# Experts' weights in pairs of units into a ring of six pairs, and the experts' outputs spread over the tokens on the chip

## The chip, the cores and the metric

One core of a Trainium2 chip. The metric is the device time of one execution in microseconds, as the median of three runs. All tensors are float32 in memory.

## The reference

Two layers of a decoder on 256 tokens of width 1024. Layer 0 is a gated DeltaNet and a dense SwiGLU, layer 1 a stick-breaking attention and a mixture of eight SwiGLU experts of which each token takes two. After each of the four parts stands a LayerNorm of `alpha * x + part(x)`. The change is in the last part:

```python
logits = xt @ router
top_val, top_idx = lax.top_k(logits, 2)
gates = softmax(top_val)
combine = sum_k(one_hot(top_idx, 8) * gates[..., None])
for e in range(8):                       # w_gate, w_up: 1024 x 3584, w_down: 3584 x 1024
    y = y + combine[:, e:e+1] * ((silu(xt @ w_gate[e]) * (xt @ w_up[e])) @ w_down[e])
h = layer_norm(alpha * h + y, g, b)
```

The experts' weights are 336 MiB.

## The kernel before

Weights come in units of 1 MiB, 128 partitions by 2048 float32. An expert is 42 units: of gate, up and down columns in four chunks (GATE, UP and DOWN give where a chunk's units stand in the round). Eight rounds run one expert each, in turn **heavy** (up to 128 rows of tokens, rounds 0, 2, 4, 6) and **light** (up to 64 rows, rounds 1, 3, 5, 7). The first heavy round is written out, then a loop of three bodies has a light and a heavy round each, and the last light round follows.

*Heavy round.* Each product is made of three f32r matmuls of high and low halves. ScalarE copies a landed unit into a high half (`hi`, line 737, and `next_hi`, 1245, six buffers), VectorE subtracts it from the unit in place, which leaves the low half in the ring (`lo`, line 2174; `los`, 2847), and TensorE multiplies (`wide_part`, 1994, `deep`, 1443; lines 1349 to 1351 are the three matmuls, 12 to a unit). TensorE's order (`heavy_round`, 2009) is gate of chunk 0 (four units), up of chunk 0 (four), two units of gate 1, `turned(0)` (transposes of silu(gate) times up, which VectorE makes in `gate_times_up`, 2835), and so on. VectorE's order is `heavy_round`, 2851: low halves 6 to 11, `gate_times_up(0)`, low half 12, ...; halves 0 to 5 are made at the end of the light round.

*Light round.* Plain fp32 matmuls straight from the landed unit, on two 64-column halves of the array at once (line 2080), with no high and low halves.

*The ring.* SyncE issues the loads in order (`units_in`, 529, issue at line 540). Twelve slots of one unit each hold the experts' weights. Unit j waits until TensorE has used unit j - 12 (`unit_used`); the first twelve wait for the dense part instead. Between the last two down chunks SyncE loads the next round's token rows from `by_slot` in HBM into `rows_io` (`slot_rows`, 518).

*Outputs.* At the start of a round ScalarE copies the round before's output out of PSUM with the gate as scale and writes it to `by_slot` in HBM (`heavy_sent`, 1206, one transfer of 512 KiB; `light_sent`, 1213, two of 128 KiB, behind four `next_hi`). When the fourth heavy output and the third light one have landed (`y_landed`), GpSimd gathers each token's two rows in four indirect transfers of 128 rows of 1024 and adds them to x (lines 697 to 719), during the last light round. The last light round's output goes another way: TensorE brings x into PSUM by the identity and adds the output by a 0/1 matrix `back` (128 rows by 256 tokens), split in Yh and Yl (`scatter`, 1973). Then the last LayerNorm (`last_norm`, 2790) reads PSUM, and five transfers store the result.

Of the kernel before, what the change touches and what calls it, by code (L numbers as in the profile page):

```python
# [21 lines left out]
ds = bass.ds  # L22
# [92 lines left out]
def hybrid_trunk(nc, x, gdn_w_in, gdn_conv_w, gdn_a_log, gdn_dt_bias, gdn_norm_w, gdn_w_out,  # L115
                 sb_w_in, sb_w_out, ffn_w_gate, ffn_w_up, ffn_w_down,
                 moe_router, moe_w_gate, moe_w_up, moe_w_down, ln_g, ln_b, out):
    with ExitStack() as ctx:
# [8 lines left out]
        raw_low = sb("raw_low", [P, RAW, UNIT], F32R, overlaid)  # L127
# [3 lines left out]
        w_lo_raw = sb("w_lo_raw", [P, SPLIT, UNIT], F32, overlaid)  # L131
        overlaid.close()
# [61 lines left out]
        def group(t, gr):  # L194
# [18 lines left out]
        w_lo_more_raw = sb("w_lo_more_raw", [P, DEEP - SPLIT, UNIT], F32, overlaid)  # L213
        overlaid.close()
# [23 lines left out]
        last_rows = ExitStack()  # L238
        Yh = sb("Yh", [P, 512], F32R, last_rows)
        Yl = sb("Yl", [P, 512], F32R, last_rows)  # L240
        last_rows.close()
# [6 lines left out]
        back = sb("back", [P, SEQ], F32R, fm)  # L248
# [29 lines left out]
        backs = sb("backs", [P, TOPK * NT], F32, fm)  # L278
        backi = sb("backi", [P, TOPK * NT], I32, fm)
# [33 lines left out]
        gdn_in = raw_in[RAW:RAW + GRAW]  # L313
        x_back = sem("x_back")
# [27 lines left out]
                  for k in range(3)]  # L342
# [28 lines left out]
        back_done, yh_done, yl_done = sem("back_done"), sem("yh_done"), sem("yl_done")  # L371
        y_sent, light_y_sent, y_landed, x_scaled, x_summed = (sem(n) for n in ("y_sent", "light_y_sent", "y_landed", "x_scaled", "x_summed"))
        y_got = [sem(f"y_got{i}") for i in range(2)]
# [18 lines left out]
        def split_slot(j):  # L392

            if U_FFN <= j < U_SBIN + 2:
                return (j + 1) % DEEP
            return j % DEEP if j >= U_MOE else j % SPLIT

        def unit_hi(j):
            s = split_slot(j)
            return w_hi[:, s, :] if s < SPLIT else w_hi_more[:, s - SPLIT, :]  # L400

        def ring_slot(j):
            return (j - U_MOE) % RING

        def ring(j, first, second, third):

            s = ring_slot(j)
            if s < RAW:
                return first[:, (s + U_MOE - U_FFN + GRAW) % RAW, :]
            return second[:, s - RAW, :] if s < RAW + SPLIT else third[:, s - RAW - SPLIT, :]  # L410

        def unit_lo(j):
            if j >= U_MOE:
                return ring(j, raw_low, w_lo, w_lo_more)
# [7 lines left out]
        def raw_slot(j):  # L422

            if j >= U_MOE:
                return ring(j, raw, w_lo_raw, w_lo_more_raw)
# [2522 lines left out]
```

## Time and profile before

| | |
|---|---|
| median of three runs | 1493.82 us (1492.81 to 1495.9) |
| the profiled execution | 1492.33 us |
| its span, first to last instruction | 1490.6 us |
| TensorE busy | 1425.4 us (96%) |
| weight loads of TensorE busy | 1054.2 us (71%) |
| VectorE, ScalarE, GpSimd busy | 831.9, 695.8, 131.3 us |
| mean granted clock of TensorE | 0.991 |
| HBM read, written | 458.03 MB, 12.34 MB |

Busy is the time in which an engine had an instruction in work. In the slices of the span each digit is tenths of one fortieth of the span (37 us). The chain of waits follows the work that ended last back from the end of the program; its rows give start, length, engine, tile and line.

### The profile page before, as it was taken

The page shows a single profiled execution, that of the slowest core. Times are in us where ns is not written, and L with a number is a line of the kernel's source. Part 1 is how long each engine was busy: PE and PEld are TensorE (multiplying, and loading weights), DVE is VectorE, ACT ScalarE, POOL GpSimd, SP SyncE. Part 2 cuts the span into 40 slices and gives each one's busy share as a digit, 9 for nine tenths or more (in the row PEclk, how much of TensorE's full clock was granted, in tenths as well). Part 3 has the DMA queues.
Part 4 walks back from the last instruction along what each step waited for, and adds up shares of the span by engine and source line. Part 5 has one row for each costly group of instructions (what it writes and reads, how often), then busy time and mean ns, then how long its engine had stood idle before and what let it go on. Part 6 is the DMA issues. An engine that isn't in the chain of part 4 may idle for free.

```text
span 1490.6 us, 19514 instructions
## 1 busy us (share of the span) xinstructions
PE 1425.4 (96%) x7640; PEld 1054.2 (71%) x7640; DVE 831.9 (56%) x739; ACT 695.8 (47%) x686; POOL 131.3 (9%) x140
## 2 busy tenths in 40 slices
PE   9999999999999999999998899997899997999976
PEld 8899988888888898888833488632688533888322
DVE  6787667644454746899700499300798102997002
ACT  6755475444333455587500587300777102875001
POOL 1668110000000000004000000000000000000021
PEclk9999999999999999999999999999999999999998
DMA  8493238565545553699999999999999999999995
GB/s 292 133 346 113 89 102 318 173 212 183 196 169 185 193 168 132 231 378 385 419 413 421 421 421 421 422 422 421 422 422 421 422 422 422 422 422 421 420 420 229
DMA packets 104389, 471.25 MB, mean 316 GB/s; under 512 B 10484, under 2 KB 17160, under 8 KB 61320
## 3 DMA queue, kind: packets, MB, share of 16 engines
q1 hardware_dynamic: 99560, 459.01, 78.0%
q10 hardware_dynamic: 3392, 7.18, 1.3%
q0 software_dynamic: 1376, 4.22, 0.7%
q8 instruction: 42, 0.69, 0.2%
q14 instruction: 19, 0.16, 0.0%
HBM read 458.03 MB, written 12.34 MB: 316 GB/s over the span
## 4 chain that ended last, share of the span: by engine, by line
PE 72%; DMA 14%; POOL 5%; DVE 5%; issue 2%; ACT 1%; SPq 1%; POOLq 0%; ACTq 0%; DVEq 0%
PE ps L1349 17%; PE ps L1351 17%; PE ps L1350 17%; PE ps L2080 10%; DMA w_lo_more_raw<-in_moe_w_down 5%; DMA raw<-in_moe_w_gate 5%; DMA raw<-in_moe_w_down 3%; POOL X L654 2%; POOL ab L649 2%; PE ps L1383 1%; PE ps L1385 1%; PE ps L1386 1%; PE ps L1669 1%; PE ps L2036 1%; PE ps L1674 1%
## 5 line engine op out<-in xcount | busy, mean ns | idle before, releaser
L762 ACT ACTIVATE w_hi<-raw 128x2048 fp32r<-128x2048 f32 x105 | 198.8, 1913 | 63.8 <-PE ps L1386 28.8
L2176 DVE TENSOR_TENSOR w_lo<-raw,w_hi 128x2048 fp32r<-128x2048 f32 x67 | 153.6, 2305 | 62.3 <-ACT w_hi L762 60.7
L2897 DVE TENSOR_TENSOR hs<-hs,ps 128x512 f32<-128x512 f32 (+1 forms) x16 | 9.9, 622 | 318.6 <-PE ps L2080 318.6
L2176 DVE TENSOR_TENSOR raw_low<-raw,w_hi 128x2048 fp32r<-128x2048 f32 x48 | 108.9, 2288 | 58.8 <-ACT w_hi L1249 49.7
L762 ACT ACTIVATE w_hi_more<-raw 128x2048 fp32r<-128x2048 f32 x62 | 117.0, 1914 | 19.1 <-PE ps L1351 16.4
L2080 PE MATMUL ps<-raw,xs_light 128*64 128x512 f32 (+1 forms) x576 | 102.5, 501 | 12.3 <-DMA raw<-in_moe_w_gate 7.9
L2176 DVE TENSOR_TENSOR raw_low<-raw,w_hi_more 128x2048 fp32r<-128x2048 f32 x48 | 108.7, 2288 | 4.9 <-ACT w_hi_more L762 3.2
L1349 PE MATMUL ps<-w_hi,xeh 128*128 128x512 f32 x224 | 91.2, 407 | 15.0 <-DVE raw_low L2176 14.7
L2080 PEld LDWEIGHTS ps<-raw,xs_light 128*64 128x64 f32 x576 | 40.2, 137 | 72.1 <-issue 46.9
L1350 PE MATMUL ps<-raw_low,xeh 128*128 128x512 f32 x224 | 90.0, 402 | 0.0
L1351 PE MATMUL ps<-w_hi,xel 128*128 128x512 f32 x224 | 89.7, 401 | 0.0
L1349 PE MATMUL ps<-w_hi_more,xeh 128*128 128x512 f32 x224 | 87.5, 391 | 0.0
L1351 PE MATMUL ps<-w_hi_more,xel 128*128 128x512 f32 x224 | 87.2, 389 | 0.0
L2176 DVE TENSOR_TENSOR w_lo<-w_lo_raw,w_hi 128x2048 fp32r<-128x2048 f32 x36 | 81.4, 2289 | 10.0 <-ACT w_hi L762 9.7
L1290 ACT ACTIVATE h_light<-ps 128x512 f32<-128x512 f32 (+1 forms) x16 | 8.7, 544 | 161.0 <-PE ps L2111 161.0
L2176 DVE TENSOR_TENSOR w_lo_more<-w_lo_more_raw,w_hi_more 128x2048 fp32r<-128x2048 f32 x36 | 81.1, 2286 | 1.7 <-ACT w_hi_more L762 1.4
L762 ACT ACTIVATE w_hi_more<-w_lo_more_raw 128x2048 fp32r<-128x2048 f32 x36 | 69.1, 1920 | 20.7 <-PE ps L1351 12.2
L762 ACT ACTIVATE w_hi<-w_lo_raw 128x2048 fp32r<-128x2048 f32 x36 | 67.9, 1912 | 13.7 <-PE ps L1351 7.5
L2080 PE MATMUL ps<-w_lo_raw,xs_light 128*64 128x512 f32 x288 | 65.0, 595 | 2.8 <-DMA w_lo_raw<-in_moe_w_up 2.8
L1383 PE MATMUL ps<-xT0h,w_hi 128*128 128x256 f32 x224 | 64.9, 290 | 0.0
L706 POOL DMA_INDIRECT rows_io<-by_slot,backi x2 | 2.0, 1004 | 710.5 <-ACTq L1223 710.2
L1385 PE MATMUL ps<-xT0l,w_hi 128*128 128x256 f32 x224 | 64.0, 286 | 0.0
(449 smaller groups left out, 3294.0 us busy)
## 6 DMA issues: line engine op xcount, KB each, us to landing
raw<-in_moe_w_gate SPq DMA_DIRECT2D x56, 1024.0 KB, 16.4
raw<-in_moe_w_up SPq DMA_DIRECT2D x56, 1024.0 KB, 17.3
raw<-in_moe_w_down SPq DMA_DIRECT2D x56, 1024.0 KB, 14.4
w_lo_raw<-in_moe_w_up SPq DMA_DIRECT2D x32, 1024.0 KB, 18.0
w_lo_more_raw<-in_moe_w_gate SPq DMA_DIRECT2D x32, 1024.0 KB, 16.8
w_lo_raw<-in_moe_w_down SPq DMA_DIRECT2D x28, 1024.0 KB, 19.4
w_lo_more_raw<-in_moe_w_down SPq DMA_DIRECT2D x28, 1024.0 KB, 23.7
w_lo_raw<-in_moe_w_gate SPq DMA_DIRECT2D x24, 1024.0 KB, 12.3
```

The lines of the kernel that those rows point to most:

```text
L649: nc.gpsimd.tensor_tensor(tmp, blocks[:, j + 1:SUB, j:j + 1].broadcast_to([P, left, j + 1]), inv[:, j:j + 1, 0:j + 1].broadcast_to([P, lef ...
L654: nc.gpsimd.tensor_tensor(rest, rest, tmp, ALU.subtract).then_inc(sub_step, 1)
L762: nc.scalar.activation(unit_hi(j), raw_slot(j), ACT.Copy).then_inc(hi_done, 1)
L1349: nc.tensor.matmul(o, lh, rh, start=start, stop=False, skip_group_check=True)
L1350: nc.tensor.matmul(o, lh, rl, start=False, stop=False, skip_group_check=True)
L1351: return nc.tensor.matmul(o, ll, rh, start=False, stop=stop, skip_group_check=True)
L1383: nc.tensor.matmul(o, unit_hi(j)[:, w], xh[:, kk, :], start=kk == 0 and m % 2 == 0, stop=False, skip_group_check=True)
L1385: nc.tensor.matmul(o, unit_hi(j)[:, w], xl[:, kk, :], start=False, stop=False, skip_group_check=True)
L1386: last = nc.tensor.matmul(o, unit_lo(j)[:, w], xh[:, kk, :], start=False, stop=kk == KD - 1, skip_group_check=True)
L1669: last = nc.tensor.matmul(ps[:, bank, h * P:(h + 1) * P], lhs(h), rhs(h), start=True, stop=True)
L2080: last = nc.tensor.matmul(ps[half * HALF:half * HALF + HALF, bank, 0:width], tile, raw_slot(j)[:, w], start=start, stop=False, skip_group_ ...
L2176: V.tensor_tensor(unit_lo(j), raw_slot(j), unit_hi(j).bitcast(F32), ALU.subtract).then_inc(lo_done, 1)
```

## The change

The ring becomes six pairs of units: HBM holds the weights so that two units stand side by side, 16 KiB per partition, and one transfer loads both when both old units are used. The twelve slots lie in one piece of memory, over `raw`, `w_hi` and `w_lo`; the experts' high halves move to `w_hi_more` and `w_lo_more`. Outputs no longer go to HBM: ScalarE leaves them in `rows_io`, VectorE builds `back` for each round, TensorE multiplies both in plain fp32 into PSUM, one token tile at a time, and VectorE adds the tile to x. The four gathers, their index steps and the Yh/Yl split go. In the last round `residual` brings x into PSUM ahead of the last two units.

```diff
-        raw_low = sb("raw_low", [P, RAW, UNIT], F32R, overlaid)
+        ring_raw = sb("ring_raw", [P, RING, UNIT], F32, overlaid)
+        overlaid.close()
+        ring_low = sb("ring_low", [P, RING, UNIT], F32R, overlaid)
...
         def unit_hi(j):
+            if j >= U_MOE:
+                s = (j - U_MOE) % DEEP
+                return w_hi_more[:, s, :] if s < SPLIT else w_lo_more[:, s - SPLIT, :]
...
-            return (j - U_MOE) % RING
-        def ring(j, first, second, third):
-            s = ring_slot(j)
-            if s < RAW:
-                return first[:, (s + U_MOE - U_FFN + GRAW) % RAW, :]
-            return second[:, s - RAW, :] if s < RAW + SPLIT else third[:, s - RAW - SPLIT, :]
+            s = (j - U_MOE) % RING
+            return (s + U_MOE - U_FFN + GRAW) % RAW if s < RAW else s
...
+        def raw_pair(j):
+            s = ring_slot(j)
+            return ring_raw[:, s:s + 2, :].rearrange("p u n -> p (u n)")
...
+            def slot_rows(r, at, light):
                 if isinstance(r, int):
                     sp.wait_ge(K_pe.sem, K_pe.after("x1", r - 1))
                 else:
-                    sp.wait_ge(light_y_sent if light else y_sent, (32 if light else 16) * (i + 1))
+                    sp.wait_ge(y_spread, NT * (r - 1))
...
             def units_in(r, u, w, e, at, first, count):
-                for i in range(count):
+                for i in range(0, count, 2):
                     j = u + at + i
                     if not isinstance(r, int) or j >= U_MOE + RING:
-                        sp.wait_ge(unit_used, units(j - RING, FC * (r - (u != U_MOE))))
+                        sp.wait_ge(unit_used, units(j + 1 - RING, FC * (r - (u != U_MOE))))
                     elif j < U_MOE + RAW:
-                        sp.wait_ge(lo_done, units(j - RAW))
-                    elif j < U_MOE + RAW + SPLIT:
-                        sp.wait_ge(unit_used, units(j - RAW - SPLIT))
+                        sp.wait_ge(lo_done, units(j + 1 - RAW))
                     else:
-                        sp.wait_ge(mixed, SBH // 2)
-                    sp.dma_start(raw_slot(j), weight_unit(w, e, first + i)).then_inc(raw_sem(j), 16)
...
-            def heavy_sent(h, r):
+            def heavy_output(h, r):
                 act.wait_ge(unit_used, units(U_MOE + DOWN[3] + 1, FC * r))
                 nc.scalar.activation(rows_io[:], ps[:, 2:4, :].rearrange("p b n -> p (b n)"), ACT.Copy,
-                                     scale=gates(heavy_meta, h)).then_inc(yh_done, 1)
-                act.wait_ge(yh_done, r + 1)
-                act.dma_start(by_slot[ds(h * PAIR + HALF, P), :], rows_io[:]).then_inc(y_sent, 16)
...
+            def light_output(l, r):
                 act.wait_ge(unit_used, units(U_MOE + DOWN[3] + 1, FC * r))
+                nc.scalar.activation(rows_io[:, 0:512], ps[:, 2, :], ACT.Copy, scale=gates(light_meta, l)).then_inc(y_copied, 1)
...
             def heavy_round(h, r, l=None):
                 if l is not None:
+                    light_output(l + 1, r - 1)
                     for k in range(2, DEEP):
                         next_hi(r, k)
-                    light_sent(l, r - 1)
                 his(r, 6, 8)
...
+            def residual():
                 for t in range(NT):
                     for half in range(2):
-                        w = slice(half * 512, half * 512 + 512)
-                        o = ps[:, 4 + 2 * t + half, :]
-                        if t == 1:
-                            nc.tensor.matmul(o, IDENT, X[:, 1, w], start=True, stop=False)
-                    pe.wait_ge(yl_done, 1)
-                    for Y in (Yh, Yl):
-                        for half in range(2):
-                            rows = slice(half * HALF, half * HALF + HALF)
-                            last = nc.tensor.matmul(ps[:, 4 + 2 * t + half, :], back[rows, t * P:(t + 1) * P], Y[rows, :],
-                                                    start=False, stop=Y is Yl)
-                            if Y is Yl:
-                                last.then_inc(y_last, 1)
+                        nc.tensor.matmul(ps[:, 4 + 2 * t + half, :], IDENT, X[:, t, half * 512:half * 512 + 512], start=True,
+                                         stop=False)
+            def spread(rows, t, o, y, start):
+                return nc.tensor.matmul(o, back[rows, t * P:(t + 1) * P], y, start=start, stop=True)
+            def heavy_spread(r, t):
+                pe.wait_ge(y_copied, r + 1)
+                pe.wait_ge(back_done, r + 1)
+                if t:
+                    pe.wait_ge(x_added, NT * r + t)
+                for half in range(2):
+                    last = spread(slice(0, P), t, ps[:, 5 + 2 * half, :], rows_io[:, half * 512:half * 512 + 512], True)
+                last.then_inc(y_spread, 1)
+            def light_spread(r, t):
+                pe.wait_ge(y_copied, r + 1)
+                pe.wait_ge(back_done, r + 1)
+                if t:
+                    pe.wait_ge(x_added, NT * r + t)
+                for half in range(2):
+                    rows = slice(half * HALF, half * HALF + HALF)
+                    last = spread(rows, t, ps[:, 6 + half, :], rows_io[rows, 0:512], True)
+                last.then_inc(y_spread, 1)
+            def last_spread(r):
+                pe.wait_ge(y_copied, r + 1)
+                pe.wait_ge(back_done, r + 1)
+                for t in range(NT):
+                    for half in range(2):
+                        rows = slice(half * HALF, half * HALF + HALF)
+                        spread(rows, t, ps[:, 4 + 2 * t + half, :], rows_io[rows, 0:512], False).then_inc(y_last, 1)
...
                 for half in range(2):
                     rows_ready(h, r, half)
                     gate(0, (2 * half, 2 * half + 1))
+                if l is not None:
+                    light_spread(r - 1, 0)
                 up(0)
+                if l is not None:
+                    light_spread(r - 1, 1)
                 gate(1, (0, 1))
+                if l is not None:
+                    pe.wait_ge(x_added, NT * r)
                 turned(0)
                 gate(1, (2, 3))
                 up(1)
                 if l is not None:
-                    pe.wait_ge(yh_done, r)
+                    pe.wait_ge(y_copied, r)
                 down(0, range(4))
                 turned(1)
                 gate(2, range(4))
                     if c:
                         pe.wait_ge(light_act.sem, light_act.after(f"high{c - 1}", l))
...
                 gate(0, range(4))
+                heavy_spread(r - 1, 0)
                 up(0)
+                heavy_spread(r - 1, 1)
                 gate(1, (0, 1))
                 turned(0)
                 gate(1, (2, 3))
                 down(1, (2, 3))
                 gate(3, range(2))
                 up(3)
+                pe.wait_ge(x_added, NT * r)
                 if not last_round:
                     heavy_rows(r + 1)
                 down(2, (0, 1))
                 turned(3)
                 down(2, (2, 3))
+                if last_round:
+                    residual()
                 down(3, range(2))
             pe.wait_ge(R_dve.sem, R_dve.after("pick1"))
...
+            def tokens_of(meta, i):
+                ids = meta[:, i, 1:2] if isinstance(i, int) else meta[:, ds(i, 1), 1:2].rearrange("p a b -> p (a b)")
+                V.tensor_scalar(back[:], tokens[:], ids, None, ALU.is_equal).then_inc(back_done, 1)
+            def output_added(r, t, banks):
+                dve.wait_ge(y_spread, NT * r + t + 1)
+                x_t = X[:, t, :].rearrange("p (b n) -> p b n", b=2)
+                V.tensor_tensor(x_t, x_t, ps[:, banks, :], ALU.add).then_inc(x_added, 1)
...
             def heavy_round(h, r):
                 first = isinstance(h, int)
-                los(h, 6, 11)
+                if first:
+                    los(h, 6, 8)
+                else:
+                    output_added(r - 1, 0, slice(6, 8))
+                    los(h, 6, 8)
+                    output_added(r - 1, 1, slice(6, 8))
+                    tokens_of(heavy_meta, h)
+                los(h, 9, 11)
                 gate_times_up(h, r, 0, slice(4, 6))
                 los(h, 12, 12)
                 if first:
...
             def light_round(l, r, last=False):
+                for t in range(NT):
+                    output_added(r - 1, t, slice(5, 8, 2))
+                tokens_of(light_meta, 0 if last else l + 1)
                 for c in range(4):
...
-            scatter_matrix()
+            tokens_of(heavy_meta, 0)
+            dve.wait_ge(x_scaled, NT)
             with dve.Fori(0, n) as i:
                 light_round(i, 2 * i + 1)
                 heavy_round(i + 1, 2 * i + 2)
             light_round(n, 2 * n + 1, last=True)
-            output_lo(2 * n + 1)
```

## Rows read from the trace of the kernel before

**Rows 1.** The page, the span in 40 slices: DMA share in tenths, GB/s.
```profile
DMA  8493238565545553699999999999999999999995
GB/s 292 133 346 113 89 102 318 173 212 183 196 169 185 193 168 132 231 378 385 419 413 421 421 421 421 422 422 421 422 422 421 422 422 422 422 422 421 420 420 229
```

**Rows 2.** Windows: stretch, length, five engines' busy us, PEclk, DMA share, GB/s.
```profile
900.00:1000.00 100.00, 100.00 (x461) 61.97 (x461) 42.75 (x24) 36.35 (x26) 0.00 (x0) 1.00 1.01 422
80.00:84.00 4.00, 4.00 (x27) 3.59 (x26) 3.94 (x3) 2.03 (x6) 0.00 (x0) 1.00 1.09 385
```

**Rows 3.** The chain of waits, from 550 us: start, us, what.
```profile
746.65 17.32 PE ps L2080 x80
...
833.53 1.92 ACT w_hi L1249
...
957.80 17.32 PE ps L2080 x80
...
1045.96 1.92 ACT w_hi L1249
...
1171.39 17.32 PE ps L2080 x80
...
1258.46 1.92 ACT w_hi L1249
...
1383.43 17.32 PE ps L2080 x80
```

**Rows 4.** Timeline of TensorE in a heavy round: units 6 and 9 begin.
```profile
855.89 0.39 PE L1349 MATMUL ps<-w_hi,xeh 128*128 128x512 f32 x1
...
864.05 0.39 PE L1349 MATMUL ps<-w_hi_more,xeh 128*128 128x512 f32 x1
```

**Rows 5.** Waits of SyncE's queue: us in total, times, longest.
```profile
SPq L540 <- PE ps L1351: 426.7, 171, 18.6
```

**Rows 6.** Line 540, whole run, then 741:747, 950:958, 1165:1172.
```profile
DMA to landing us min/median/max: 4.7/16.0/29.4
...
DMA to landing us min/median/max: 6.1/6.3/6.6
...
DMA to landing us min/median/max: 9.0/9.1/9.5
...
DMA to landing us min/median/max: 7.5/8.0/8.4
```

**Rows 7.** DMA issues: count, KB each, median us to landing.
```profile
by_slot<-rows_io ACTq DMA_DIRECT2D x4, 512.0 KB, 7.9
...
by_slot<-rows_io ACTq DMA_DIRECT2D x6, 128.0 KB, 6.7
...
rows_io<-by_slot,backi POOLq DMA_INDIRECT x2, 8.8
hs<-by_slot,backi POOLq DMA_INDIRECT x2
```

**Rows 8.** Timeline of TensorE in `scatter`.
```profile
1475.66 1.98 PE L1977 MATMUL ps<-X,cst 128*128 128x512 f32 x4
...
1477.57 0.49 PE L1989 MATMUL ps<-Yh,back 64*128 64x512 f32 x2
```

**Rows 9.** VectorE's lines 2839, 2783, 2176: ns min/median/max.
```profile
L2839 DVE TENSOR_TENSOR hs<-hs,ps x16: 679/1213/1216, 650.8 to 1366.3; 128x1024 f32<-128x1024 f32 x12, 128x512 f32<-128x512 f32 x4
...
L2783 DVE TENSOR_SCALAR back<-tokens,light_meta x1: 353/353/353, 737.4 to 737.4; 128x256 fp32r<-128x256 f32 x1
...
L2176 DVE TENSOR_TENSOR raw_low<-raw,w_hi x48: 2281/2291/2294, 601.1 to 1360.4; 128x2048 fp32r<-128x2048 f32 x48
```

**Rows 10.** Timeline of the tail: last unit, its copy, statistics of tile 1.
```profile
1473.79 1.94 PE L2080 MATMUL ps<-w_lo_more_raw,h_light 128*64 128x512 f32 x8 [0.51 <-DMA w_lo_more_raw<-in_moe_w_down]
...
1475.77 0.69 ACT L1201 ACTIVATE Yh<-ps,light_meta 128x512 fp32r<-128x512 f32 x1 [9.16 <-PE ps L2080]
...
1480.91 0.70 DVE L2795 BATCH_NORM_STATS2 stats<-ps 128x6 f32<-128x512 f32 x1 [0.97 <-PE ps L1989]
```

More of the change, by code:

```diff
@@ L370, in hybrid_trunk @@
         K_dve = Stages(sem("K_dve"), ["l0", "l1"])
-        back_done, yh_done, yl_done = sem("back_done"), sem("yh_done"), sem("yl_done")
-        y_sent, light_y_sent, y_landed, x_scaled, x_summed = (sem(n) for n in ("y_sent", "light_y_sent", "y_landed", "x_scaled", "x_summed"))
-        y_got = [sem(f"y_got{i}") for i in range(2)]
+        back_done, y_copied, y_spread, x_scaled, x_added = (sem(n) for n in ("back_done", "y_copied", "y_spread", "x_scaled",
+                                                                            "x_added"))
         def by_halves(at):
@@ L402, in ring_slot @@
         def ring_slot(j):
[L403 to L410 removed]
+            s = (j - U_MOE) % RING
+            return (s + U_MOE - U_FFN + GRAW) % RAW if s < RAW else s
         def unit_lo(j):
             if j >= U_MOE:
[L414 removed]
+                return ring_low[:, ring_slot(j), :]
             s = split_slot(j)
@@ L558, in expert @@
                 if at is not None:
-                    next_rows(r, i, at, light)
+                    next_rows(r, at, light)
                 units_in(r, u, moe_w_down, e, DOWN[2], 8, 4)
@@ L755, in hi @@
                     act.wait_ge(unit_used, units(U_SBIN - 2 if j == U_SBIN + 2 else U_SBIN - 1))
-                elif j < U_MOE + SPLIT and first:
+                elif j < U_MOE and first:
                     act.wait_ge(unit_used, units(j - SPLIT))
@@ L1321, in _ @@
             n = act.value_load(idi[0:1, COUNT:COUNT + 1], min_val=BODIES, max_val=BODIES + MAX_OVER)
-            with act.Fori(n, TURNS):
-                act.sem_inc(y_landed, 2)
             with act.Fori(0, n) as i:
@@ L1327, in _ @@
             light_round(n, 2 * n + 1, last=True)
-            act.wait_ge(unit_used, units(U_MOE + DOWN[3] + 1, FC * (2 * n + 1)))
-            last_output()
+            light_output(0, 2 * n + 1)
             nc.scalar.activation(warm[:, 3], rw[:, 0, 0:1], ACT.Sqrt, scale=0.0)
@@ L1971, in first_rows @@
                 last.then_inc(K_pe.sem, 1)
-            def scatter():
-                pe.wait_ge(x_summed, TOPK * NT)
-                for half in range(2):
-                    nc.tensor.matmul(ps[:, 4 + half, :], IDENT, X[:, 0, half * 512:half * 512 + 512], start=True, stop=False)
-                pe.wait_ge(back_done, 1)
+            def residual():
                 for t in range(NT):
                     for half in range(2):
-                        w = slice(half * 512, half * 512 + 512)
-                        o = ps[:, 4 + 2 * t + half, :]
-                        if t == 1:
-                            nc.tensor.matmul(o, IDENT, X[:, 1, w], start=True, stop=False)
-                    pe.wait_ge(yl_done, 1)
-                    for Y in (Yh, Yl):
-                        for half in range(2):
-                            rows = slice(half * HALF, half * HALF + HALF)
-                            last = nc.tensor.matmul(ps[:, 4 + 2 * t + half, :], back[rows, t * P:(t + 1) * P], Y[rows, :],
-                                                    start=False, stop=Y is Yl)
-                            if Y is Yl:
-                                last.then_inc(y_last, 1)
+                        nc.tensor.matmul(ps[:, 4 + 2 * t + half, :], IDENT, X[:, t, half * 512:half * 512 + 512], start=True,
+                                         stop=False)
@@ L2878, in heavy_round @@
                 los(h, 26, 28)
-                if first:
-                    outputs_placed()
                 los(h, 29, 32)
```

105 lines of the change are left out of this document (24 added, 81 removed), and 2 rows, old and new, of the table R_dve.

## The prediction

> **What bounds the kernel now.** I read the page's slices first [rows 1]: in the experts' half, from about 690 us on, the DMA engines stand at 9 in every slice and move 413 to 422 GB/s, while TensorE's row also shows 9. Two engines that both look full call for a view by stage. A stretch inside the experts (first row of [rows 2]) has DMA at a share of 1.01 and 422 GB/s, so 1 MiB takes 2.49 us. The chain of waits [rows 3] shows how the two share the time. A heavy round runs from the moment its first unit has landed (833.53, 1045.96, 1258.46) to the first matmul of the next light round (957.80, 1171.39, 1383.43): 124.3, 125.4 and 125.0 us, mean 124.9. One heavy unit is 2.72 us of TensorE (three from 855.89 to 864.05 [rows 4]), more than the 2.49 us in which a unit arrives, so TensorE falls behind the stream. A light unit is 1.73 us (17.32 us for 80 matmuls, ten units [rows 3]), so there TensorE catches up and waits for data: from 957.80 to the next landing at 1045.96 are 88.2 us. The period, one light and one heavy round, is 212.4 us. The transfers of a period (84 units, 0.75 MiB of rows in, 0.75 MiB of outputs out) at 2.49 us are 212.9: the stream is never interrupted.
>
> How near it is to an interruption is what decides this change. SyncE waited 426.7 us for the heavy rounds' matmuls [rows 5]: each transfer is issued when TensorE frees a slot, so the ring of 12 is always full and the room left is the time from issue to landing. With nothing ahead of it a unit lands after 4.7 us (first of [rows 6]), 2.49 of transfer and about 2.2 of latency. At the end of the heavy rounds that time falls to 6.1 us in the first one, then 9.0 and 7.5 [rows 6]: only some 3 to 4 us of slack are left before the DMA engines would idle.
>
> **The change part by part.** *Traffic that goes.* Four heavy outputs of 512 KiB, six light pieces of 128 KiB [rows 7] and four gathers of 128 rows of 4 KiB (0.5 MiB each) are 4.75 MiB: 11.8 us at 2.49, if the stream never stops. That is a ceiling, not the result; 1.9 us of it lies in each period.
>
> *Rows of 16 KiB instead of 8.* No row shows such a transfer. In a stretch with packets of about 1 KiB the engines, as full, moved 385 GB/s, in the experts with 8 KiB 422 [rows 2]: 2.72 against 2.49 us per MiB with 64 against 8 packets per engine, 0.24/56 = 4.3 ns a packet. Four packets less per MiB give 0.02 us. The lower bound is no gain or, by other strides in memory, a small loss; the upper one 0.04, if a packet costs twice that. I take 0.02, so 2.47 per MiB: 5.7 us over the 284 units that follow the first heavy round, again only if the stream never stops.
>
> The Trainium skill, DMA: Bandwidth & Descriptors, section Measured, tells to batch, with 341 GB/s at 1 MB and 425 at 16 MB, and would promise far more from pairs. Here 1 MiB transfers already run at 422 GB/s [rows 2], since others are queued behind them, so that rule has nothing left to give. The Trainium skill, DMA: Bandwidth & Descriptors, section Where 436 GB/s comes from, sets a ceiling of 435 GB/s, an estimate of 2.41 us per MiB; were it reached, the total below would be some 8 us lower.
>
> *Pairs.* Unit 0 of a heavy round now lands with unit 1, 2.47 us later against the stream, and with it all of the round. A slot is refilled only when both its units are used, and the pair then needs 4.94 + 2.2 = 7.1 us to land. Before, a slot's second unit landed 7.5 to 9.0 us after it was issued; that leaves 0.4 to 1.9 us, less than the 2.47 just added. So pairs alone stop the stream at each heavy round's end.
>
> *Spreading a light output, in the heavy round.* Four logical fp32 matmuls of 64 rows by 512. Two logical ones of 128 rows took 1.98 us, and two f32r ones on different 64-row halves overlapped, 0.49 us for both [rows 8]. So a token tile costs 0.98 us if halves overlap and 1.96 if not; I take 0.98 by the overlap shown, 2.0 us per heavy round. TensorE is the late one there, so nothing hides it. VectorE gets waits that stand ahead of the low halves: output_added(0) waits for the first spread (after four units) ahead of los 6 to 8, output_added(1) for the second (after eight) ahead of los 9 to 11 and gate_times_up(0), which TensorE's turned(0) needs. From the end of the second spread: X add 1.21, tokens 0.35, low half of unit 9 2.29 [rows 9], ready at about 3.95 with the gaps. TensorE was done with unit 8 at 2.72: 1.2 us lost. Two more low halves and the product (2.2 + 2.2 + 1.2) end at 9.7, while TensorE finishes unit 9 at 6.7: 3.0 us lost. Together 4.2; bounds 0 (if VectorE were let ahead) and 5. A heavy round with a light one before it is thus 2.0 + 4.2 = 6.2 us longer.
>
> *Spreading a heavy output, in the light round.* 2 x 1.96 = 3.9 us of TensorE and two adds on VectorE, where TensorE waits for data: nothing, as 42 x 1.73 + 3.9 is below the 88. ScalarE's light_output now stands ahead of four high halves, but it is due 2 us before their units land: nothing. Meta and index steps that go were beside other work. SyncE's wait for y_sent becomes one for y_spread, due earlier in its queue: nothing. At the start, the last three pairs wait for the last unit of the dense part, yet the heavy round needs them ten units later: nothing.
>
> *The sum.* With the stream stopped at a heavy round's end T, the pair issued at T lands at T + 7.1; fifteen more and the next heavy round's first follow at 4.94, plus 0.5 MiB of rows: T + 7.1 + 79.0 + 1.2 = T + 87.3 (88.2 before). Heavy: 124.9 + 6.2 = 131.1. Period 218.4 against 212.4. From T = 746.65, the first light matmul [rows 3]: heavy unit 0 at 833.9; T = 965.0; then +218.4 twice: 1183.4, 1401.8. The last light round needs 7.1 + 15 x 4.94 = 81.2 to its last landing: 1483.0. Before it was 1473.7 [rows 10]: 9.3 us later.
>
> *The tail.* Before, from the last landing to the statistics of tile 1 on VectorE are 1480.9 - 1473.7 = 7.2 us [rows 10]. After: the second last pair landed 4.9 us earlier and takes 3.7, done at -1.2; residual() then puts 3.9 us of fp32 matmuls ahead of down(3), to +2.7; two units, +6.3; copy 0.8, first spread 1.1, +8.2; two statistics and their moments 1.6, +9.8. So 2.6 us later, although the two residual pairs and the low half of Y went: moved ahead, they meet the last pair's wait of 1.4 us, not an empty engine. Sum 9.3 + 2.6 = 11.9. The profiled execution took 1492.33 us (span 1490.6 plus 1.7), so 1504.2; it stood 1.5 below the median of the runs, 1493.82, which gives 1505.7. The chained bounds lean both ways; I say 1505.
>
> **Rivals.** (1) *Faster: the stream never stops.* If the heavy rounds stay ahead of the ring (slack after the change above 7.1 us from issue to landing), all savings count: -11.8 - 5.7 + 2.6 = -14.9, some 1479. For it: the bytes are counted, DMA is full now. Against: the slack of 7.5 to 9.0 [rows 6], less than what the change adds (2.5 + 6.2 and a stream that runs 3.6 us per period earlier). It decides from about 9 us more of slack per heavy round. (2) *No change: VectorE's waits don't bite.* Without the 4.2 us, three times, 1505 - 12.6 = 1492. For it: VectorE is idle part of a heavy round; against: the program order, which has no way round. (3) *More: the 64-row halves don't overlap.* 2.0 us more in each of three heavy rounds, 1511. For it: no fp32 row shows the overlap. (4) *The change doesn't do what it says*: 16 KiB rows run no better, or slower. A loss of 0.02 per MiB instead of the gain is 0.04 x 32 units x 4 = 5 us, 1510.
>
> **How the numbers follow.** Forecast 0.64, rival 1 0.13, rival 2 0.08, rivals 3 and 4 0.15 together. The range reaches over the last three, 1488 to 1513; below it lies rival 1 and above it a few in a hundred. About 0.2% is what can be told from no change. Rival 1 and part of rival 2 make faster 0.16; same 0.07; slower 0.77. The forecast's own range is 1499 to 1511.
>
> **What would show it.** Right: DMA share below 0.97 in the last 15 us of each heavy round of the profile after, and issue to landing near 7.1 us there; 131 us from a heavy round's first landing to its end; TensorE waiting for w_lo or the product around its tenth unit; a period near 218; four IDENT matmuls ahead of the last two units. Wrong: a DMA share of 1.0 throughout with a period near 208 (rival 1); a heavy round of 127 (rival 2); or light rounds that take longer than 88 us.

## The result, and the profile after

The changed kernel takes 1515.34 us (1511.93 to 1516.93, 4 runs) against 1493.32 of the kernel before (1491.91 to 1495.9, 4 runs) on the same chip: a ratio of 1.0137 [1.0124, 1.0151] (the bracket is the 95% interval), so 20.4 us slower. The forecast was slower by 12, with a range that ended at 1513. One execution of e1 below took 3745.66 us, two and a half times as long as all others, and is in no ratio. The profiled execution took 1514.19 us, its span 1510.9 against 1490.6: 20.3 us to account for.

The page of the changed kernel, its span in 40 slices, beside [rows 1]:

```profile
DMA  8493238555555543799999999999989999999995
GB/s 288 135 339 113 86 111 306 196 209 179 173 212 183 183 167 113 280 372 396 416 429 426 428 379 384 382 429 429 429 334 383 391 429 429 429 349 385 397 428 218
```

Before, the rate was 420 to 422 in every slice from 745 us to the last but one. Now it is 426 to 429 in the light rounds and falls to 334 to 397 in the heavy ones behind them: the stream of transfers is interrupted in every period. The share of the DMA engines hardly tells; it is still 9 in all but one of these slices. Windows of the same kernel (columns as in [rows 2]), from a heavy round into the light one behind it:

```profile
850.00:950.00 100.00, 96.61 (x436) 78.08 (x435) 87.72 (x46) 73.21 (x43) 0.00 (x0) 1.00 0.98 389
950.00:960.00 10.00, 10.00 (x48) 8.27 (x47) 4.09 (x3) 1.22 (x3) 0.00 (x0) 1.00 0.92 365
...
970.00:980.00 10.00, 10.00 (x44) 3.21 (x42) 1.22 (x1) 0.60 (x1) 0.00 (x0) 1.00 1.00 426
980.00:1050.00 70.00, 63.24 (x322) 24.21 (x318) 5.17 (x8) 4.84 (x9) 0.00 (x0) 1.00 1.01 429
```

Finer windows show where it begins. In the second heavy round, behind the stall of VectorE's order that the chain shows below:

```profile
1098.00:1100.00 2.00, 2.00 (x8) 1.56 (x7) 2.00 (x2) 2.00 (x2) 0.00 (x0) 0.72 0.96 410
1100.00:1102.00 2.00, 2.00 (x10) 1.64 (x9) 2.00 (x2) 1.41 (x2) 0.00 (x0) 1.00 0.41 172
1102.00:1104.00 2.00, 2.00 (x10) 1.68 (x9) 2.00 (x3) 1.22 (x1) 0.00 (x0) 1.00 0.04 16
1104.00:1106.00 2.00, 2.00 (x10) 1.65 (x10) 2.00 (x2) 1.92 (x1) 0.00 (x0) 1.00 0.77 139
```

The waits of SyncE's queue in 1085:1110 (total us, times, longest) say why: no slot was free.

```profile
SPq L528 <- PE ps L1292: 27.3, 4, 10.1
```

The queue waited 10.1 us for TensorE's matmuls of a heavy pair. For about 2 us next to nothing moves (16 GB/s), and from there to the round's end the rate comes and goes with TensorE's pace. In the kernel before no window of 2 us in the three heavy rounds behind a light one was under 401 GB/s.

The chain of waits of the changed kernel, its lines that answer to [rows 3] (w_hi_more at L1196 is a heavy round's first high half, L2042 the light units, L1921 a spread, L1992 turned()):

```profile
744.78 7.02 PE ps L2042 x32
...
834.43 1.92 ACT w_hi_more L1196
...
851.96 1.06 PE ps L1921 x4
...
864.14 1.08 PE ps L1921 x4
...
866.74 2.21 DVE ring_low L2143
...
872.01 2.56 issue
874.57 1.06 PE ps L1992 x8
...
965.47 7.02 PE ps L2042 x32
...
1055.32 1.92 ACT w_hi_more L1196
...
1188.36 7.02 PE ps L2042 x32
...
1278.42 1.92 ACT w_hi_more L1196
...
1409.30 7.02 PE ps L2042 x32
```

Heavy rounds: 131.0, 133.0 and 130.9 us (124.3, 125.4, 125.0 before). Light rounds, from the first light matmul to the next heavy landing: 89.65, 89.85, 90.06 (86.9, 88.2 and 87.1 before, by [rows 3]). From issue to landing, line 528 (the pairs), in the stretches 945:957, 1165:1175 and 1375:1390, in or at the end of a heavy round, beside [rows 6]:

```profile
DMA to landing us min/median/max: 9.0/9.3/9.7
...
DMA to landing us min/median/max: 8.6/8.8/8.9
...
DMA to landing us min/median/max: 8.7/9.1/9.8
```

These are pairs with at most one other pair still under way; the forecast had 7.1. Over the three heavy rounds, from behind the stall to the first light matmul, the 45 pairs took 8.0 to 10.4 us, 9.7 in the middle. The pair issued at the first light matmul itself, the T of the forecast's sum, is the one that matters. The stretches 965:967 and 1188:1190 hold it alone:

```profile
DMA to landing us min/median/max: 10.0/10.0/10.0
...
DMA to landing us min/median/max: 10.2/10.2/10.2
```

In the first light round it took 9.8.

The waits of TensorE in 834:966 show what stands in the heavy round, and the timeline the tail, beside [rows 10]:

```profile
PE ps L1290 <- DVE ring_low L2143: 6.3, 2, 5.5
PE ps L1992 <- issue: 2.6, 1, 2.6
```

The wait of 5.5 us is that for the round's first high and low half; e3, without the stall, has it too. What VectorE's new order adds is the other wait of 0.8 and the 2.6 for the product.

```profile
1486.91 3.65 PE L2042 MATMUL ps<-ring_raw,h_light 128*64 128x512 f32 x16 [0.78 <-DMA ring_raw<-in_moe_w_down]
1490.49 3.70 PE L1917 MATMUL ps<-X,cst 128*128 128x512 f32 x8
1494.12 3.65 PE L2042 MATMUL ps<-ring_raw,h_light 128*64 128x512 f32 x16
...
1501.25 0.64 DVE L2756 BATCH_NORM_STATS2 stats<-ps 128x6 f32<-128x512 f32 x1
```

The residual's matmuls for both tiles (3.70 us together) stand between the last two pairs. The last pair was issued at 1466.6 and landed 25.1 us later, at 1491.7, and waits for TensorE till 1494.12.

### The profile page after: what moved, and what is told of

It is laid out like the page before. It is cut to its first block, busy times and chain, and to the rows that moved or that the text cites. A ratio compares the mean times of both kernels' runs of the same rounds, so it can differ in the third digit from the quotient of the medians.

```text
span 1510.9 us, 19084 instructions
## 1 busy us (share of the span) xinstructions
PE 1442.5 (95%) x7696; PEld 1067.4 (71%) x7696; DVE 848.4 (56%) x756; ACT 694.1 (46%) x686; POOL 117.8 (8%) x132
## 4 chain that ended last, share of the span: by engine, by line
PE 75%; DMA 10%; POOL 5%; DVE 5%; issue 2%; ACT 1%; POOLq 0%; DVEq 0%; SPq 0%; ACTq 0%
PE ps L1290 17%; PE ps L1292 17%; PE ps L1291 17%; PE ps L2042 11%; DMA ring_raw<-in_moe_w_gate 5%; DMA ring_raw<-in_moe_w_down 5%; POOL X L642 2%; POOL ab L637 2%; PE ps L1921 2%; PE ps L1324 1%; PE ps L1326 1%; PE ps L1327 1%; PE ps L1610 1%; PE ps L1992 1%; DVE ring_low L2143 1%
## 5 line engine op out<-in xcount | busy, mean ns | idle before, releaser
L2143 DVE TENSOR_TENSOR ring_low<-ring_raw,w_hi_more 128x2048 fp32r<-128x2048 f32 x84 | 189.4, 2288 | 60.0 <-ACT w_hi_more L1196 50.8
L2042 PE MATMUL ps<-ring_raw,xs_light 128*64 128x512 f32 (+1 forms) x1024 | 198.4, 542 | 9.8 <-DMA ring_raw<-in_moe_w_up 5.2
L2143 DVE TENSOR_TENSOR ring_low<-ring_raw,w_lo_more 128x2048 fp32r<-128x2048 f32 x84 | 189.0, 2287 | 6.1 <-ACT w_lo_more L726 4.6
L1291 PE MATMUL ps<-ring_low,xeh 128*128 128x512 f32 x448 | 177.2, 396 | 0.0
L2042 PEld LDWEIGHTS ps<-ring_raw,xs_light 128*64 128x64 f32 x1024 | 73.2, 137 | 130.1 <-issue 115.2
L726 ACT ACTIVATE w_lo_more<-ring_raw 128x2048 fp32r<-128x2048 f32 x75 | 143.2, 1918 | 39.7 <-PE ps L1292 38.9
L726 ACT ACTIVATE w_hi_more<-ring_raw 128x2048 fp32r<-128x2048 f32 x75 | 142.2, 1915 | 41.5 <-PE ps L1292 27.1
L2042 PE MATMUL ps<-ring_raw,h_light 128*64 128x512 f32 x448 | 102.1, 597 | 16.6 <-DMA ring_raw<-in_moe_w_down 14.6
L1291 PEld LDWEIGHTS ps<-ring_low,xeh 128*128 128x128 f32 x448 | 86.2, 192 | 17.4
L1290 PE MATMUL ps<-w_lo_more,xeh 128*128 128x512 f32 x224 | 88.8, 396 | 2.5 <-DVE ring_low L2143 2.5
L1292 PE MATMUL ps<-w_lo_more,xel 128*128 128x512 f32 x224 | 87.6, 391 | 0.0
L2042 PEld LDWEIGHTS ps<-ring_raw,h_light 128*64 128x64 f32 x448 | 33.0, 137 | 74.3 <-issue 69.4
```

What stands on the lines that cost most here:

```text
L726: nc.scalar.activation(unit_hi(j), raw_slot(j), ACT.Copy).then_inc(hi_done, 1)
L1290: nc.tensor.matmul(o, lh, rh, start=start, stop=False, skip_group_check=True)
L1291: nc.tensor.matmul(o, lh, rl, start=False, stop=False, skip_group_check=True)
L1292: return nc.tensor.matmul(o, ll, rh, start=False, stop=stop, skip_group_check=True)
L2042: last = nc.tensor.matmul(ps[half * HALF:half * HALF + HALF, bank, 0:width], tile, raw_slot(j)[:, w], start=start, stop=False, skip_group_ ...
L2143: V.tensor_tensor(unit_lo(j), raw_slot(j), unit_hi(j).bitcast(F32), ALU.subtract).then_inc(lo_done, 1)
```

## The experiments

Theory A: the slower time is the loss of the ring's slack, from three sources: pairs that land late on an emptied queue, spreads that stretch the heavy round, the residual in the tail. The rivals (B to H, each told in the expectation of the run that tests it) put it on one part alone, or on another mechanism. All ratios are to the kernel before, timed beside each run on the same chip; its medians were 1495.28 (e1 to e4), 1495.75 (e5 to e8) and 1495.51 (e9, e10), so the ratios compare, not the medians.

Nor do the totals of single traces compare. The first light matmul stands at 744.8 to 746.7 us in five of the twelve (both kernels, e1, e4, e7), where TensorE's granted clock in 150:200 was 1.00, and at 748.9 to 750.6 in the other seven, where it was 0.92 to 0.95: up to 5.8 us, before any light round and without a pattern by the edit. So what follows compares rounds within the traces, and totals by the ratios.

**e1, outputs on the chip, but single units.** The ring has 12 slots of 1 MiB again, each with its own wait and semaphore:

```diff
...
-sp.dma_start(raw_pair(j), weight_pair(w, e, (first + i) // 2)).then_inc(raw_sem(j), 16)
+sp.dma_start(raw_slot(j), weight_unit(w, e, first + i)).then_inc(raw_sem(j), 16)
...
```

> The changed kernel with the ring of 12 single units put back (8 KiB rows, one slot refilled as soon as its unit is used); the outputs stay on the chip. Theory A (the pairs take away the ring's slack, and a pair that starts on an empty queue needs 8.6 us to land): the pairs cost most of the 20 us, so some 1490 us here, a light round of about 85 us and the last 15 us of the heavy rounds near the ring's limit but with single units landing in 4.7 to 6 us; the heavy rounds stay near 129 us from first landing to end, since VectorE's stall is still there. Theory B (the spreads are what costs, pairs are harmless): 1508 to 1515, as the changed kernel.

1500.72 us, ratio 1.0029 [1.0013, 1.0046]. Pairs thus cost 1.1% of the change's 1.4%, but the rest is no gain: theory A had said 1490. The heavy rounds took 132.9, 132.75 and 133.0 us where 129 was expected, the light ones 86.1, 85.8 and 85.3. Some 2 us of each heavy round are a drop of TensorE's clock behind the stall, told at the end. A unit landed in 4.6 to 5.3 us at the heavy rounds' ends: the ring is run empty with units too, only at a lower price.

**e2, pairs alone, in the kernel before.** The ring, the waits for two units and the place of the high halves are those of the change:

```diff
...
-sp.dma_start(raw_slot(j), weight_unit(w, e, first + i)).then_inc(raw_sem(j), 16)
+sp.dma_start(raw_pair(j), weight_pair(w, e, (first + i) // 2)).then_inc(raw_sem(j), 16)
...
```

> The kernel before with the ring of six pairs alone; outputs still go through HBM and the four gathers. Theory A: the heavy round keeps its 125 us, the light round and the step to the heavy one grow to about 90 us, in all 1500 (6 to 8 us slower than before), with the DMA share below 1 at the end of the heavy rounds. Theory B: at 429 GB/s in place of 422 it is 5 to 8 us faster than before, 1487.

1503.22 us, ratio 1.0058 [1.0040, 1.0076]. With heavy rounds as before (124.9, 125.1, 125.1) the light ones grew to 90.9, 89.75 and 89.9: pairs hurt by themselves, through landings of 7.7 to 10.8 us at the ends of the heavy rounds. The two parts alone cost 0.58% (e2) and 0.29% (e1), together 1.37%, more than their sum: they draw on the same slack.

**e3, spreads early.** Each light spread goes two gate units forward, where VectorE's queue has not yet reached the low halves of the next units:

```diff
                     gate(0, (2 * half, 2 * half + 1))
-                if l is not None:
-                    light_spread(r - 1, 0)
+                    if l is not None:
+                        light_spread(r - 1, half)
                 up(0)
-                if l is not None:
-                    light_spread(r - 1, 1)
```

> The changed kernel with light_spread(0) after the second gate unit and light_spread(1) after the fourth, each two to four units earlier, so that VectorE adds the outputs before it is needed for low halves 6 and 9. Theory A: TensorE's stall around its tenth unit goes, 3 to 4 us in each of three heavy rounds, and since the ring is the limit all of it counts: 1503 to 1505, heavy rounds of 127.5 us. Rival C (TensorE's lag in the heavy round is made up in the light round, where it waits for data anyway): within 2 us of 1515.

1501.52 us, ratio 1.0045 [1.0029, 1.0061], 13.7 us under the changed kernel by the ratios and 1.5 below what theory A said. The heavy rounds fell to 126.9, 127.75 and 126.7, so the order of the spreads, not their number, made 4.2 of the 6.2 us. The light rounds stayed at 88.9, 89.7 and 89.45. Its chain of waits, in which the low half and the wait behind it no longer stand:

```profile
838.05 1.92 ACT w_hi_more L1196
...
849.83 1.06 PE ps L1921 x4
...
856.57 1.06 PE ps L1921 x4
...
964.91 7.02 PE ps L2040 x32
```

**e4, residual early.** In the last round residual(0) stands before down(2, (0, 1)), residual(1) before down(2, (2, 3)).

```diff
+                if last_round:
+                    residual(0)
                 down(2, (0, 1))
                 turned(3)
+                if last_round:
+                    residual(1)
                 down(2, (2, 3))
-                if last_round:
-                    residual()
                 down(3, range(2))
```

> The changed kernel with the identity matmuls of the last round split: tile 0 ahead of down(2, (0, 1)), tile 1 ahead of down(2, (2, 3)). Theory A: they fill waits of 1.2 us per pair, the last two units start when they land, 2 to 3 us less: 1512.5. Rival D (they only shift the wait): 1515.

1513.16 us, ratio 1.0123 [1.0092, 1.0154]: 2.1 us less by the ratio, but the intervals overlap, so the time alone can't tell it from nothing. The traces can. From the last round's first light matmul to the copy of its output (`rows_io`) the changed kernel took 88.5 us and e4 86.6:

```profile
1491.28 7.06 PE ps L2042 x32
...
1498.36 0.70 ACT rows_io L1174
```

residual(1) now runs before it, at 1489.56, and the last four units follow in one go. The other pairs of traces with the late and the early order agree: e3 89.1 and e10 86.8, e1 86.1 and e8 83.5. Theory A's 2 to 3 us are there, 2.0 to 2.5; the total hid them, as e4's three heavy rounds (133.5, 132.85, 133.0) all had the clock drop and only one of the changed kernel's did.

**e5, two transfers per pair.** Slots are refilled in pairs, each pair by two 1 MiB transfers with a semaphore each:

```diff
...
-                        sp.wait_ge(unit_used, units(j - RING, FC * (r - (u != U_MOE))))
+                        sp.wait_ge(unit_used, units(j + 1 - i % 2 - RING, FC * (r - (u != U_MOE))))
...
```

(These lines are against e1.)

> The changed kernel with pairs only as the unit of refilling: both units are issued when both old ones are used, but as two transfers of 1 MiB with 8 KiB rows and a semaphore each. Theory A (the long landing of a pair on an empty queue, and that its first unit is usable only with its second): the first unit lands after 4.7 us and the second after some 7.1, so light rounds near 86 us and 1502 to 1505 in all, between the ring of single units (1498) and the changed kernel (1514). Rival G (only the later refill costs, not the pair's own landing): as the changed kernel, 1512 to 1515.

1507.46 us, ratio 1.0080 [1.0057, 1.0103], between e1 and the changed kernel and 2.5 us above theory A's range: of the 16 us between these two about half is the late refill, about half the long transfer. The split is rough, since e1's trace has three clock drops, this one none and the changed kernel's one; the light rounds bear it out: 86.1, 85.8 and 85.3 in e1, here 88.5, 87.9 and 87.4, with the long transfer 89.65 to 90.06. The long transfer differs from these two in its single notice and in its rows; e6 parts them. At 1375:1390 the units land after 4.8 to 7.2 us, the second of a pair some 2 us behind the first:

```profile
DMA to landing us min/median/max: 4.8/6.0/7.2
```

**e6, one transfer per pair, 8 KiB rows.** A pair is one 2 MiB transfer again, but its rows in HBM are the units' rows of 8 KiB.

```diff
...
-return w[ds(e * (MOE_UNITS // 2 * P) + i * P, P), :]
+return w[ds((e * (MOE_UNITS // 2) + i) * 2 * P, 2 * P), :].rearrange("(u p) n -> p u n", p=P)
...
```

> The changed kernel with one 2 MiB transfer per pair, but in rows of 8 KiB (the units one behind the other in HBM). If the 16 KiB rows make a pair land late on an empty queue (9 us where 7.1 was reckoned), it lands here in 7.1 us and the whole takes 1506 to 1508, the saturated rate falling back from 429 to 422 GB/s. If it is the transfer's size whatever its rows, 9 us stay and the time is 1515 to 1518.

1519.36 us, ratio 1.0163 [1.0145, 1.0180]. The landing went as the first branch said, the time as neither (1506 to 1508, 1515 to 1518). The landing at 1375:1390, and that of the pair issued at the second round's T (974:976):

```profile
DMA to landing us min/median/max: 7.4/7.4/7.5
...
DMA to landing us min/median/max: 7.2/7.2/7.2
```

So 7.1 was about right for 2 MiB in rows of 8 KiB. The 45 pairs of the same stretches took 7.2 to 9.4 us, 7.5 in the middle, against 9.7 with rows of 16 KiB. Much of that gap needs another pair under way. Where the queue had run empty or nearly so behind the stall, a pair of 16 KiB rows landed after 7.7, 8.1 and 8.7 us (issued at 881.3, 1104.2 and 1325.1) and 7.6 (e9, at 1106.9), one of 8 KiB rows after 7.4, 7.5 and 7.4 (e6, at 889.8, 1111.5 and 1333.5). The full gap is there when another pair was issued 5.3 to 6.5 us before.

The light rounds answer to it. At the second and third T a pair landed after 7.2 and 7.6 us and the rounds took 88.3 and 88.7, 1.6 and 1.3 less than in the changed kernel; at the first it took 9.6, for a reason left open, and the round 90.55. The total went the other way. The full stream runs at 422 again, not 429, and all three heavy rounds took 133.1 to 133.4, with the clock drop in each; and this trace is one of those with the late start, 5.6 us behind the changed kernel's, which the edit did not make. The windows of e1 show such a drop:

```profile
872.00:874.00 2.00, 1.55 (x8) 1.58 (x9) 2.00 (x2) 0.00 (x0) 0.00 (x0) 0.54 1.02 426
874.00:876.00 2.00, 2.00 (x8) 1.62 (x7) 2.00 (x2) 1.57 (x2) 0.00 (x0) 0.61 1.00 418
```

**e7, spreads doubled.** As e3, but each light spread is issued twice.

```diff
                 for half in range(2):
                     rows = slice(half * HALF, half * HALF + HALF)
+                    spread(rows, t, ps[:, 6 + half, :], rows_io[rows, 0:512], True)
+                for half in range(2):
+                    rows = slice(half * HALF, half * HALF + HALF)
                     last = spread(rows, t, ps[:, 6 + half, :], rows_io[rows, 0:512], True)
```

> The changed kernel with the light spreads moved two to four units ahead as before, and each of them issued twice (same operands, same result). Theory A (TensorE's lag in a heavy round counts in full, since the ring is full): 2.1 us more in each of three heavy rounds than with the spreads once, 1501.5 + 6.4 = 1508. Rival C (the light round makes it up): 1501.5.

1504.84 us, ratio 1.0075 [1.0058, 1.0092]: 4.5 us over e3 by the ratios, whose intervals just touch, between theory A's 6.4 and rival C's nothing. The heavy rounds grew by 2.4, 1.9 and 1.5 us (2.1 more TensorE work in each), the two later light ones shrank by 1.5 and 1.0. TensorE's extra work in a heavy round counts nearly in full there, and part of it comes back behind it.

**e8, all mended.** e1, e3 and e4 together.

> The changed kernel's outputs on the chip, with the ring of 12 single units, the light spreads moved ahead and the identity matmuls of the last round moved ahead. Theory A: the heavy round is 127 us and the stream of transfers runs on, or nearly so, at 422 GB/s with 4.75 MiB less to move; the ring's slack of about 3 us per heavy round takes 2.1 of TensorE and 1.9 of the lighter traffic, so 1482 to 1486 in all, 8 to 11 us faster than before. Theory B (the spreads are too much for TensorE however placed): 1494 or slower.

1485.29 us (1479.1 to 1487.43, 6 runs), ratio 0.9932 [0.9911, 0.9953]: 10 us faster than the kernel before, the best version. Heavy rounds 127.65, 127.4, 127.4; light ones 85.7, 84.5 and 84.3. Its chain of waits and its windows:

```profile
962.38 7.02 PE ps L2044 x32
...
1046.92 1.92 ACT w_hi_more L1200
...
1174.30 7.02 PE ps L2044 x32
```

```profile
940.00:950.00 10.00, 10.00 (x48) 8.26 (x47) 8.63 (x5) 6.42 (x5) 0.00 (x0) 1.00 1.02 422
950.00:960.00 10.00, 10.00 (x48) 8.28 (x47) 1.01 (x2) 0.60 (x1) 0.00 (x0) 1.00 0.99 387
960.00:970.00 10.00, 10.00 (x45) 4.29 (x44) 0.00 (x0) 1.67 (x2) 0.00 (x0) 1.00 1.00 383
...
980.00:1040.00 60.00, 58.51 (x307) 22.28 (x308) 5.16 (x8) 4.84 (x9) 0.00 (x0) 1.00 1.01 422
```

The stream is short only in the last 15 us or so of the heavy round (420 GB/s over 840:940), where the changed kernel ran at 389 over a hundred. This is the picture that the prediction had of the changed kernel itself.

**e9, 16 KiB rows at a pitch of 17 KiB.** The weights are padded in HBM, so that the partitions' rows do not stand a power of two apart.

```diff
...
-                return w[ds(e * (MOE_UNITS // 2 * P) + i * P, P), :]
+                return w[ds(e * (MOE_UNITS // 2 * P) + i * P, P), 0:2 * UNIT]
...
+    return np.pad(a, ((0, 0), (0, 256)))
```

> The changed kernel with 1 KiB of padding behind each 16 KiB row of the experts' weights in HBM; as many bytes are loaded, in rows of 16 KiB at a pitch of 17 KiB. If the pitch is why a pair of 16 KiB rows lands after 8.8 us on an empty queue where 8 KiB rows do in 7.5 (e6), it lands in about 7.3 here, the light rounds shrink by 1.4 us and the time is 1508. If the long rows themselves are why, nothing moves: 8.8 us and 1513 to 1516.

1512.97 us, ratio 1.0112 [1.0095, 1.0129]. The landings stayed, at 1165:1175:

```profile
DMA to landing us min/median/max: 8.8/8.9/8.9
```

Over the 45 pairs they were 7.8 to 10.4 us, 9.5 in the middle (9.7 without padding), and the light rounds 89.3, 89.4 and 88.4. The pitch is not the cause of the late landing. Why long rows land some 2 us later when another pair is under way stays open.

**e10, pairs with both orders mended.** e3 and e4 together, pairs kept.

> The changed kernel with both orders mended (light spreads and identity matmuls moved ahead) and the pairs kept; beside the run with single units (1485) it gives the price of the pairs once nothing else is in the way. Theory A (the ring's slack pays for pairs whatever else is mended): 1498 to 1500, 13 to 15 us above the single units. Rival H (without VectorE's stall there is slack enough for the pairs, and their 429 GB/s begins to count): 1485 or below.

1497.58 us, ratio 1.0013 [0.9999, 1.0027]. With e8 it completes a square:

| | orders as changed | orders mended |
|---|---|---|
| pairs | 1.0137 | 1.0013 (e10) |
| single units | 1.0029 (e1) | 0.9932 (e8) |

Pairs cost 1.08% and 0.81%, the orders 1.24% and 0.97%. With units and both orders, 10.2 of the 11.8 us that the outputs' bytes are worth come out as a gain. The early residual has a part in it, 2.0 to 2.5 us by the traces (e4). The heavy rounds of e8 are 5.4 us shorter than those of e1; some 2 us of that are the clock drop, which went with the stall.

## Why the prediction was right in direction and wrong in size

**What bounds it: right.** The ring's slack decides, not the bytes. e1 and e2 each take away a part of the change and each stays slower than before, though each moves no more bytes than before. (At the end of the first heavy round the slack before was only 1.4 us, 6.1 against 4.7, not the forecast's 3 to 4.) Rival 1 (the stream never stops) is refuted by the windows. The stop comes earlier than was said: not in the last 15 us of a heavy round, but behind its stall, 85 to 88 us before its end (880, 1100 and 1322 against 965.47, 1188.36 and 1409.30). That costs nothing more: TensorE was busy without a gap from 876 to 966, and the heavy rounds took what the sum gave them; what is left at the end is a ring with one pair under way, nearly as forecast.

**VectorE's order: right.** 4.2 us of stall were forecast for a heavy round with a light one before it. The chain shows the low half at 866.74 and 2.56 us of waiting at 872.01, where 3.0 was said (the other wait was 0.8, not 1.2). The heavy rounds took 131.0 and 130.9 where 131.1 was said, and e3, which moves only the spreads, gave back 4.2, 5.3 and 4.2, in the second round with the clock drop. Rival 2 fell.

**The overlap of 64-row halves: right.** A light spread took 1.06 us per token tile against 1.91 for a heavy one. Rival 3 fell.

**The tail: right.** From the last landing at 1491.7 to tile 1's statistics at 1501.25 are 9.5 us; 9.8 was said.

**The step that failed** is a term of the sum: "the pair then needs 4.94 + 2.2 = 7.1 us to land". It had been put together from the slope of a full queue and the latency of a single 1 MiB transfer, as if the stream stood still at T. Measured for just this pair were 9.8, 10.0 and 10.2 us. The rest of each light round, fifteen pairs, the rows and the next first pair, took 79.7 in all three where 80.2 was said, so each light round took 89.65 to 90.06 us instead of 87.3, and that one term holds all of the excess. At T the pair before was still under way: issued at 960.2 it landed at 968.2, 2.7 us behind T.

Three light rounds are 7.7 us of the 8.7 that the sum fell short by. The rest: heavy rounds +1.6 (one had the clock drop told below), the last light round +1.3, the start -1.9. The kernel is then 11.9 + 8.7 = 20.6 us slower, less 0.3 of the tail; 20.3 are measured. e6 isolates the term: the same 2 MiB in rows of 8 KiB lands in 7.2 and 7.6 us at two of three such places, also with a pair under way, and the light round shrinks with it. So it is long rows behind another pair that add the rest. (One reading of the forecast was off without touching the sum: its 88.2 us for a light round before is the longest of three, whose mean is 87.4.)

**The rate of long rows: mis-sized, and of little use.** 2.47 us per MiB were taken against 2.49. In the full stream the pairs ran at 429 GB/s (430 in e2), which is 2.44, twice the gain. It counts only where the stream is full, and there the landing took it back. The gain is that of the rows, not of the size: e6 moves 2 MiB at a time in rows of 8 KiB, and its full stream ran at 422. The Trainium skill, DMA: Bandwidth & Descriptors, section Measured, advises to batch transfers to 1 MiB or more, and its table rises from 341 GB/s at 1 MB to 425 at 16 MB. In this case's full queue no such rise shows from 1 to 2 MiB (422 and 422), and going on to pairs loses: e10 against e8 is 12 us slower, since a pair is issued later, tells of its end later and, with its long rows, lands later.

**Rivals 3 and 4** came nearest with 1511 and 1510 against 1515, each for a reason that is refuted: the halves overlap, and long rows move more in a full stream.

Left open: why long rows land late behind another pair, and what decides whether the clock drops behind the stall.

## What to carry to other kernels

Where a ring is full and its refills wait for the consumer, measure the slack as the time from issue to landing where it is shortest, compare it with that of a transfer on an empty queue, and add up what a change takes from it. Measure a new transfer's landing with another under way, too: that is how it is met when the ring runs low (9.7 us against 7.7 to 8.7 here). And bytes saved are only worth something while slack is left. Larger transfers shrink it three ways: they are issued later, take longer, and report only at their end. Work added to an engine that is late counts nearly one for one in its stage, and some two thirds of it in the end here (4.5 of 6.4 us, e7). A wait added to a queue that runs in order costs whatever stands behind it, so place it where that queue has not yet been asked for anything: the two spreads placed two and four units earlier turned, with the tail's order, a loss of 0.3% (e1) into a gain of 0.7% (e8).

## What the runs showed of the hardware

2 MiB transfers in rows of 16 KiB ran at 429 GB/s in a full queue against 422 in rows of 8 KiB (with 1 MiB or 2 MiB transfers), yet when the queue was nearly drained, each pair issued 5.3 to 6.5 us behind another, they landed after 8.0 to 10.4 us (9.7 in the middle) against 7.2 to 9.4 (7.5). On a queue run empty or nearly so it was 7.6 to 8.7 against 7.4 and 7.5. The DMA share is a poor sign of an interrupted stream: over 10 us or more it stood at 0.92 to 0.98 where the rate had fallen from 429 to 365 and 389, and at 1.00 where it was 383 (e8). The rate is the column to read.

TensorE's granted clock could drop behind a short stall. It did so at the head of heavy rounds in both kernels, after some 5 us of waiting (0.50 in 840:842 here, in 1052:1054 before), and could do so behind the stall of 2.56 us. In the changed kernel's second heavy round, that of 133.0 us:

```profile
1095.00:1097.00 2.00, 1.10 (x6) 1.13 (x7) 2.00 (x2) 0.00 (x0) 0.00 (x0) 0.67 1.00 426
1097.00:1099.00 2.00, 2.00 (x8) 1.71 (x8) 2.00 (x2) 1.12 (x2) 0.00 (x0) 0.50 1.02 434
```

The clock is at its lower level, 1.2 GHz, for some 3 us, and turned() takes 1.94 us there instead of 1.06. In the first heavy round, with the same 2.56 us of waiting for the product, it stayed at 1.00:

```profile
874.00:876.00 2.00, 1.43 (x11) 1.37 (x12) 2.00 (x2) 0.33 (x1) 0.00 (x0) 1.00 0.98 418
```

Rounds with the drop took 132.75 us and more, those without 130.5 to 131.0 (the changed kernel, e5 and e9): some 2 us each, once in the changed kernel, in two rounds of e9, in all three of e1, e4 and e6, in none of e5, and in none of e3, where the stall is gone. What decides it stays open.
